# A three-block network on one core: third feed-forward layer with one whole block pair, norms by columns, third activation sum behind the first whole tile

## The reference

```python
x = x + concat(mix_out, mem_out) @ w_out            # layers 0, 1
x = x + conv_ffn(rmsnorm(x, norm_ffn_g[l]), ...)    # u, g = split(h @ w_up); g = causal_dwconv(g); (silu(g) * u) @ w_down
...
h2 = rmsnorm_2(x, norm2_g)                          # the third feed-forward layer
x = x + (silu(h2 @ w_gate) * (h2 @ w_up)) @ w_down  # w_gate, w_up: 1024 x 2816, w_down: 2816 x 1024
return rmsnorm_2(x, normf_g)

def rmsnorm(x, g): return x * rsqrt(mean(x * x, axis=-1) + eps) * g
```

## Time and profile before

| | us |
|---|---|
| median of 3 runs | 1789.06 (1788.8 to 1791.18) |
| the profiled execution | 1791.19 |
| its span | 1789.5 |
| PE busy | 1771.5 (99%) |
| DVE busy | 1280.6 (72%) |
| ACT busy | 943.4 (53%) |
| POOL busy | 211.8 (12%) |
| granted clock of PE, mean | 0.998 |

### The profile page before, as it was taken

One profiled execution on the slowest core, in us unless ns is written; L12 is line 12 of the kernel. 1 busy time (PEld: TensorE's weight loads), 2 busy tenths in 40 slices (PEclk: granted clock), 3 DMA queues, 4 the chain that ended last, 5 costly groups with the idle time before them and its releaser, 6 DMA issues.

```text
span 1789.5 us, 26202 instructions
## 1 busy us (share of the span) xinstructions
PE 1771.5 (99%) x10677; PEld 1529.5 (85%) x10677; DVE 1280.6 (72%) x1774; ACT 943.4 (53%) x1425; POOL 211.8 (12%) x229
## 2 busy tenths in 40 slices
PE   9999999999999999999999999999999999999998
PEld 7877788999999787887899999977777879999996
DVE  6878567888786756556888788687767577776765
ACT  5645444655555545655465555553567446454454
POOL 2001220110111200002011010103001101111110
PEclk9999999999999999999999999999999999999999
DMA  6122223555544333212364554443221235555452
GB/s 247 55 94 77 71 94 106 147 138 141 142 127 133 106 122 113 95 50 71 106 175 120 153 129 134 115 118 106 72 95 48 78 123 142 142 141 142 109 146 65
DMA packets 60871, 205.19 MB, mean 115 GB/s; under 512 B 7232, under 2 KB 9408, under 8 KB 52048
## 3 DMA queue, kind: packets, MB, share of 16 engines
q1 hardware_dynamic: 38080, 162.55, 27.3%
q0 software_dynamic: 17280, 31.46, 9.9%
q10 hardware_dynamic: 5392, 9.51, 1.7%
HBM read 169.38 MB, written 2.13 MB: 96 GB/s over the span
## 4 chain that ended last, share of the span: by engine, by line
PE 84%; DVE 8%; ACT 5%; DMA 1%; issue 1%; POOL 1%; SPq 0%; ACTq 0%; DVEq 0%; POOLq 0%
PE ps L1709 28%; PE ps L1376 19%; PE ps L1735 16%; PE ps L1395 5%; PE ps L1310 3%; PE ps L1764 2%; DVE WL L2376 2%; PE ps L1522 2%; PE ps L1567 2%; PE ps L1547 2%; PE ps L1415 1%; ACT WH L1840 1%; PE ps L1606 1%; DMA raw<-in_wall 1%; ACT hH L2178 1%
## 5 line engine op out<-in xcount | busy, mean ns | idle before, releaser
L2376 DVE TENSOR_TENSOR WL<-raw,WH 128x1024 fp32r<-128x1024 f32 (+1 forms) x140 | 171.6, 1266 | 106.0 <-ACT WH L1840 106.0
L2398 DVE TENSOR_TENSOR WL<-raw,WH 128x1024 fp32r<-128x1024 f32 x135 | 164.9, 1222 | 115.2 <-ACT WH L1851 115.2
L1709 PE MATMUL ps<-hH,WH 128*128 128x256 f32 x864 | 244.7, 283 | 1.4 <-ACT held L1916 1.4
L1709 PE MATMUL ps<-hH,WL 128*128 128x256 f32 x864 | 244.5, 283 | 0.0
L1709 PE MATMUL ps<-hL,WH 128*128 128x256 f32 x864 | 244.5, 283 | 0.0
L1376 PE MATMUL ps<-hH,WH 128*128 128x512 f32 x592 | 235.5, 398 | 3.1 <-DVE hL L2343 2.7
L1376 PE MATMUL ps<-hH,WL 128*128 128x512 f32 x592 | 230.7, 390 | 0.0
L1376 PE MATMUL ps<-hL,WH 128*128 128x512 f32 x592 | 230.6, 390 | 0.0
L3146 POOL DMA_DIRECT2D X<-sq x120 | 105.0, 961 | 861.0 <-ACT sq L1901 858.9
L1709 PE MATMUL ps<-TH,WL 128*128 128x256 f32 x648 | 183.4, 283 | 0.0
L1709 PE MATMUL ps<-TL,WH 128*128 128x256 f32 x648 | 183.4, 283 | 0.0
(11 more groups left out here) (419 smaller groups left out, 3888.6 us busy)
## 6 DMA issues: line engine op xcount, KB each, us to landing
raw<-in_wall SPq DMA_DIRECT2D x162, 512.0 KB, 4.3
raw<-in_wall SPq DMA_DIRECT2D x68, 1024.0 KB, 4.8
X<-sq POOLq DMA_DIRECT2D x120, 256.0 KB, 3.9
bias<-in_bias ACTq DMA_DIRECT2D x12, 256.0 KB, 3.0
X<-in_xt SPq DMA_DIRECT2D x8, 256.0 KB, 8.6
CB<-rows ACTq DMA_DIRECT2D x8, 256.0 KB, 3.4
raw<-in_wall SPq DMA_DIRECT2D x4, 256.0 KB, 5.2
mrA<-in_memt ACTq DMA_DIRECT2D x4, 256.0 KB, 5.7
```

What stands on the lines that cost most here:

```text
L1709: mm = e.matmul(ps[b][:, 256 * u:256 * u + 256], ww[:, p, 128 * u:128 * u + 128], x, start=(opens and p == 0 and u == 0 and n == 0), stop= ...
L2376: e.tensor_tensor(WL[v][:, c], unit_raw(n)[:, c], WH[v][:, c].bitcast(F32), ALU.subtract).then_inc(*mark("wl", n, x))
L2398: e.tensor_tensor(L, chunk_src(c), H.bitcast(F32), ALU.subtract).then_inc(*mark("wl", "c", c))
```

## The change

Five things: (a) `WHOLE` becomes (2, 2, 1): the third layer computes its second block pair by seven products. `SEQUENCE` is one list for each layer; the third layer's begins q1, q5, q6 of pair 1, d of group 0, q3, q7, q2, q1 of pair 2, q4. (b) In all three feed-forward layers the norm goes by columns: `rstd_first` stands after the first gate tile and `rstd_second` after the second; the diagonal is made on ACT. (c) The step `wtS` with p = 1 no longer stands ahead of the last output tile but after the first gate tile. (d) `wtL` with p = 3 stands ahead of the two `wu0`. (e) At the end of layer 0, POOL's adds of squares 5 to 7 wait for the last `hL`.

```diff
-WHOLE = 2
+WHOLE = (2, 2, 1)
-T_SUMS = {4: (("wtB", 0), ("wtS", 0)), 5: (("wtL", 0), ("wtB", 1)), 6: (("wtS", 1),)}
+T_SUMS = {4: (("wtB", 0), ("wtS", 0)), 5: (("wtL", 0), ("wtB", 1))}
...
         elif s == 1:
-            out += [q[1], q[2], d[0], q[5], q[6], q[3], q[7], ("q", 2, 1), q[4]]
+            out += [q[1], q[5], q[6], d[0], q[3], q[7], q[2], ("q", 2, 1), q[4]]
...
         whole("g", 0, n)
-        put("rstd_rows", st, 61 if i == 2 else 60)
+        put("rstd_first", st, 61 if i == 2 else 60)
+        put("wtS", i, 1)
         put("wtL", i, 1)
         put("wtB", i, 2)
         put("wtS", i, 2)
         whole("g", 1, n)
         done.add(n)
+        put("rstd_second", st)
...
         conv_ahead(len(UNITS))
         put("wtS", i, 3)
+        put("wtL", i, 3)
         put("wu0", f"u{i}", 0)
         put("wu0", f"u{i}", 1)
-        put("wtL", i, 3)
-        for s in range(1, WHOLE):
+        for s in range(1, WHOLE[i]):
...
-        later([], [("wu0", f"u{i}", 2 * WHOLE - 1)], [("wt7", i)], [("wlast", i, WHOLE - 1)])
-        for x in SEQUENCE:
+        if WHOLE[i] == 2:
+            later([], [("wu0", f"u{i}", 3)], [("wt7", i)], [("wlast", i, 1)])
+        else:
+            put("wlast", i, 0)
+            later([("wt7", i)])
+        for x in SEQUENCE[i]:
...
                     e.activation(small[:, 0:4], ps[BANK[("rs", a[0])]][:, 0:4], ACT.Sqrt, bias=small[:, eps:eps + 1],
                                  scale=1.0 / 1024).then_inc(*mark("rsq", a[0]))
+                    if a[0] in WINO_OF:
+                        w.wait_ge(*at("rcol", a[0]))
+                        w.wait_ge(*at(*DIAG_BEFORE[a[0]]))
+                        for n in range(4):
+                            e.activation(diag[:, n * 128:n * 128 + 128], ident, ACT.Copy,
+                                         scale=small[:, 4 + n:5 + n]).then_inc(*mark("diagA", a[0], n))
...
-                    w.wait_ge(*at("rrow", FFN_NORM[i]))
+                    w.wait_ge(*at("Rsb", FFN_NORM[i]))
...
+                        if m > 4:
+                            w.wait_ge(*at("hL", "mix1", 7))
                         e.tensor_tensor(acc[:, :], acc[:, :], sq[m % 2][:, :], ALU.add).then_inc(
                             *mark("accP", st, m))
```

More of the change, by code:

```diff
@@ L66, in part_tiles, with wino_sequence @@
     return range(4 * c, 4 * c + 4) if g == 0 else range(2 * c, 2 * c + 2)
-def wino_sequence():
-    out = []
-    if WHOLE == 2:
-        out.append(("d", 0, 0))
-    for s in range(WHOLE, NSU):
+def wino_sequence(whole):
+    out = [("d", 0, 0)] if whole == 2 else []
+    for s in range(whole, NSU):
         q = {n: ("q", s, n) for n in PRODUCTS}
         d = [("d",) + x for x in down_pieces(s)]
-        if s < WHOLE:
-            continue
-        if s == 2 and WHOLE == 2:
+        if s == 2 and whole == 2:
             out += [q[1], q[5], q[6], q[3], d[0], q[7], q[2], q[4]]
         elif s == 1:
-            out += [q[1], q[2], d[0], q[5], q[6], q[3], q[7], ("q", 2, 1), q[4]]
+            out += [q[1], q[5], q[6], d[0], q[3], q[7], q[2], ("q", 2, 1), q[4]]
         elif s == 2:
@@ L91, in wino_sequence @@
     return out
-SEQUENCE = wino_sequence()
+SEQUENCE = [wino_sequence(x) for x in WHOLE]
 def wino_plan(up, upo, gate, gateo, down, idx, i):
     out, roles = [], []
-    for s in range(WHOLE):
+    for s in range(WHOLE[i]):
         out += [(gate, idx, 0, 8, gateo + 256 * s, 256), (up, idx, 0, 8, upo + 256 * s, 256)]
-    keys = list(dict.fromkeys(SEQUENCE))
+    keys = list(dict.fromkeys(SEQUENCE[i]))
     def needs(x):
@@ L177, in chunk_list @@
         seen.add(i)
-        for key in dict.fromkeys(SEQUENCE):
+        for key in dict.fromkeys(SEQUENCE[i]):
             c = {"key": (i,) + key, "i": i, "sum": None, "unit": None}
@@ L655, in ffn_wino @@
                 put("wc11", i, s)
-            if q == (3 if s == 1 and WHOLE == 1 else 2):
+            if q == 2:
                 put("wgr", i, s)
@@ L2579, in vector @@
                 elif what == "rstd_second":
-                    diagonal(a[0], small[:, 4:8], ("rcol", a[0]))
+                    if a[0] not in WINO_OF:
+                        diagonal(a[0], small[:, 4:8], ("rcol", a[0]))
                 elif what == "last_sums":
```

20 lines of the change are left out of this document (11 added, 9 removed).

## The result

| | before | changed |
|---|---|---|
| median of the runs | 1789.68 us (1788.8 to 1791.18, 4 runs) | 1797.62 us (1796.31 to 1798.53, 4 runs) |
| ratio to before | | 1.0041, 95% interval 1.0029 to 1.0052 |
| profiled execution: own time, span | 1791.19, 1789.5 us | 1797.66, 1795.9 us |

The change makes the kernel slower by 7.9 us in the medians and by 6.4 us in the spans of the two profiles. With the experiments the kernel before was run many more times; its medians there were 1790.1 to 1790.6 us, which puts the loss at 7.0 to 7.5 us. The profiled execution of the kernel before (1791.19) lies above all of these medians, so a difference of two profiles can be off from that of the medians by a microsecond or so.

What follows compares the result with a forecast made beforehand. PE's own work bounds the kernel, busy 1771.5 of 1789.5 us. Terms -1.6 + 2.5 - 3.4 - 0.7 + 0.6 + 6.9 + 1.0 = +5.3 us, put on the 1789.06 median: 1794.4 us, range 1789.5 to 1798.

Steps and rivals of the forecast that it cites:

- rival C: Third layer: the clock falls and stays low beyond q6, each further product adding 2.9 us; usual size 1797 us; chance 0.2.
- the sum p = 1: Starts of the three layers: moved behind the first gate tile, it removes waits for `hL` and POOL's last add; gain 3.4 us.
- the end of layer 0: PE resumes 1.4 us earlier, then waits for a low weight part held up behind POOL's adds; loss 0.6 us.
- The new wait: Third layer, pair 1: q5 waits 3.4 us for `TL` p = 3, q6 3.4 for q1's copy; 6.9 us with slower restart.
- R: Third layer: start on ACT of the conversion that waits for the end of the first up tiles; 1454.30 before.
- The clock: Third layer: the nearly idle stretch may bring the lower clock for the products behind it; 1.0 us, bounds 0 and 2.9.
- The products: Third layer's second pair: seven products take 20.1 us of PE where the whole pair took 21.8; saving 1.6 us.
- the norm: Three feed-forward layers: by columns it costs PE 0.84 us more in each, 2.5 us in all, with no wait.
- Layer 1's q3: Layer 1: q3's wait of 0.62 us for the copy of q5 goes, its work starting earlier; gain 0.7 us.
- Rivals A: Third layer, q5 and q6 of pair 1: the wait does not arise or is under 1 us; 1786.5 us; chance 0.1.
- B: Third layer: the wait is there but the clock stays up; +4.3, 1793.4 us; chance 0.28.
- D: End of layer 0 or layer 1's spread product: diagonal or weights come late; +1 to +2 us, 1796; chance 0.1.

Runs made afterwards that it cites:

- early sum: Changed kernel with the third layer's last sum of activations and its low half put ahead of the conversions that wait for the up tiles: 1792.99 us, ratio 1.0016.
- early copy: Changed kernel with the copy of product 1 ahead of the first pair's last activations on ScalarE, the last sum still late: 1792.74 us, ratio 1.0015.
- filled waits: Changed kernel with product 5 of the third layer's first odd pair computed nearly three times over, 42 products more within the two waits: 1794.79 us.
- gate off: Changed kernel without the wait that keeps POOL's last three sums of squares of layer 0 behind the last low half: 1795.08 us, ratio 1.0028.
- the norms alone: Kernel before with the norms by columns in the three layers and nothing else of the change: 1792.15 us, ratio 1.0008.
- both early: Changed kernel with the last sum early and the copy of product 1 ahead of the first pair's last activations: 1788.7 us, ratio 0.9992.
- the version in which VectorE's queue had been filled: Changed kernel with last sum and copy of q1 moved ahead, only POOL's last two adds held back: 1787.71 us; with norms by rows again 1795.62 us.

## Why the prediction was right, and where a size was off

Forecast 1794.4 us in a range of 1789.5 to 1798; measured 1797.62, only 0.4 us inside the upper bound. The side and the deciding mechanism were right; the sum was +5.3 us and the spans show +6.4, the medians +7.9 (7.0 to 7.5 against the longer series of the kernel before). The number is nearer to rival C's 1797 than to the forecast, though what C says did not happen. By place, the third layer came out 1.4 us over its share of the sum and layer 1 0.8 over; the sum p = 1 gave 0.3 more than forecast, the end of layer 0 cost 0.3 less, and 0.5 of the last stretch belongs to no term.

- **The new wait, +6.9.** Right in place, in makers and in size. q6 was to start at R + 12.3 and started at R + 12.32, and q5 started 9.64 us before it, where 9.7 were named. Had q1 and q5 run through, their 48 matmuls from 1453.28 on would have ended at 1459.04; q6 started 6.76 us later. The split was to be 3.4 and 3.4 us and was 3.23 and 2.44, since q5's last quarter at the lower clock filled 0.94 us of the second. The early sum and the early copy take the two waits away one at a time.
- **The clock, +1.0.** This is the term that was mis-sized. It measured 2.40 us, by the filled waits and by q6's own length, and 1.47 in the other profile of the same third layer (gate off). The upper bound of 2.9 was itself too high: all of q6 lay at the lower clock, and its matmuls then took 0.22 us each against 0.120, less than double. The 1.0 was a choice between 0 and 2.9 and not a reading, since no row had a wait of that length with work behind it. The Trainium skill ("TensorE: Matmul & The Clock Gate", Part 1) has the fall to 1.2 GHz behind idling as the rule, and the trace of the changed kernel agrees here; that of the early sum, with 3.02 us of idling and no fall, does not. Rival C, the clock low beyond q6, did not come: the clock was back as q6 ended.
- **The products, -1.6, and the norm, +2.5.** The third layer gives -1.6 + 0.8 + 6.8 + 2.4 = +8.4 with the waits and the clock as measured, against +8.57, so the two sizes fit there; neither was measured by itself. Over the three layers the norms alone cost 1.9 us in the medians, 0.92 of it in the third layer of the profile.
- **The sum p = 1, -3.4.** Right. The waits for `hL` and POOL are gone, and the three places gave 0.5 us (first stretch), 1.6 (218.69 against 220.27 with the gate off; in the changed kernel the new wait for weights hides it) and 1.6 (start of the third layer, 88.71 against 90.28). But "Next late in that place is nothing that I see" was true of the place and not of the layer: without the norm by columns layer 1 gives 3.0 us back further on.
- **Layer 1's q3, -0.7.** This did not come. Layer 1 by itself, from its sums to the next norm's, takes 356.32 us instead of 355.42, which is the norm's 0.8 and no gain. q3's wait did shrink, from 0.62 us to 0.25, but a later product's wait for its copy grew from 0.39 to 0.80. First the kernel before, then two rows of the changed one:

```profile
928.30 0.39 PE L1709 MATMUL ps<-hH,WH 128*128 128x256 f32 x1 [0.39 <-ACT held L1916]
```

```profile
898.73 0.39 PE L1711 MATMUL ps<-hH,WH 128*128 128x256 f32 x1 [0.25 <-ACT held L1918]
...
928.29 0.39 PE L1711 MATMUL ps<-hH,WH 128*128 128x256 f32 x1 [0.80 <-ACT held L1918]
```

- **The end of layer 0, +0.6.** PE did wait for the low weight part, 1.50 us against some 2, and resumed behind the last `hL` at 617.82 instead of 618.75. The mechanism, with POOL's end at 622.0 and ScalarE's loads behind it, is the one that was forecast. It is partly luck that it showed: with the same code the profile of the filled waits has no wait there. That such a wait can bring the lower clock, some 1.5 us more in other profiles, I had not counted.
- **Rivals A** (no wait) and **B** (clock up) are out by the trace, and so is **D**: in no layer did the product with the diagonal wait. Rival A's kernel is the one with both early, whose 1788.7 us lies 2 us above the 1786.5 I had given it; 1.0 of that is the down piece's wait.

## What to carry to other kernels

When a step is moved ahead of other work, follow the in-order queues of the engines that feed it, and look for an instruction that waits for the bottleneck engine itself: everything behind it starts only at that point, however idle the engine was before. Here DVE stood 4.62 us with the needed sum queued behind such a wait, and moving it into the gap, together with one copy, gave 9 us. Test an edit with its partners as well as alone: the norm by columns cost 1.9 us by itself and was worth 7.9 us in the version in which VectorE's queue had been filled.
